# First unit after norms 2 to 6 multiplied with the channel-scaled residual; last two down-projections in one accumulation

## The chip, the cores and the metric

One core of a Trainium2 chip runs the whole program. The metric is the device time of one execution in microseconds (us). The kernel before was timed three times on the chip; one further execution was profiled.

## What is computed

Two layers over 512 tokens (256 latent, 256 context) of 1024 channels, all in float32:

```python
def rms_norm(x, w):
    y = xf * rsqrt(mean(xf * xf, axis=-1) + EPS)      # EPS = 1e-6
    return y * w
def modulate(h, shift, scale): return h * (1 + scale) + shift
def swiglu(h, w13, w2):
    g, u = split(h @ w13, 2)                           # D_FF = 2816
    return (silu(g) * u) @ w2
# per layer, the same weights for latent and context tokens, shift/scale/gate per stream:
x = x + 0.5 * gate1 * swiglu(modulate(rms_norm(x, w1), shift1, scale1), w13a, w2a)
x = x +       gate2 * mixer (modulate(rms_norm(x, w2), shift2, scale2))
x = x + 0.5 * gate3 * swiglu(modulate(rms_norm(x, w3), shift3, scale3), w13b, w2b)
```

The mixer projects to 2576 columns, runs differential attention, windowed attention and a two-directional state-space scan, and projects back. There are six norms: norm 1 at the start, norm 2 before mixer 0, norm 3 before FFN 1, norm 4 before FFN 2, norm 5 before mixer 1, norm 6 before FFN 3. In the code they are n = 0 to 5.

## The kernel before

Tokens lie along the free axis: a tile is 128 channels by 512 tokens, and 1024 channels are KT = 8 tiles, `k` or `d`. Every weight comes as a unit of 128 x 2048 numbers (256 output columns for 8 channel tiles, or 256 hidden rows for a down-projection). SyncE loads a unit into `raw`; ScalarE rounds it to fp32r, `w_hi` (`split`, L527 to L539); VectorE takes the rest, `w_lo` (L872 to L880). TensorE forms each product with three matmuls: high by high, high by low, low by high (`mm3`, L1417). Three slots of `w_hi` and `w_lo` are used in turn.

An FFN has 11 pairs of units: gate, up and down. Gate goes to PSUM banks 0 and 1, up to banks 2 and 3, down to banks 4 to 7 (`4 + d % 4`, so that down tile d + 4 waits until VectorE has added tile d to the residual `x_res`, `update`, L975). The first gate and up units of an FFN stand ahead of its loop (L1449 and L1450). TensorE then runs gate 1, down 0, up 1 and so on. FFN 0 to 2 have 512 tokens, FFN 3 has the 256 latent ones.

A norm runs like this. ScalarE squares a residual tile as soon as it is updated (`norm_square`, L548); VectorE adds the squares (`add_square`, L939). After the last projection one matmul with a matrix of 1/1024 gives the mean in bank 0 (`mean`, L1441). ScalarE loads the table for Ln and Exp, computes the root (L566, L568). Then for each of the 8 tiles VectorE multiplies by the root (L957), ScalarE applies scale and shift for each stream and rounds (L576, L579), and VectorE takes the remainder (L950). TensorE's next unit starts tile by tile as the remainders come.

The order of the work on ScalarE, VectorE and TensorE in a mixer is written out by hand in `WEAVE`, one list for each layer; each engine goes through the list and does what is its own, so an engine that waits holds up all that stands behind it. The lists begin as follows (`T` a projection tile on TensorE, `E` its evacuation by ScalarE, `cv` a convolution on VectorE in five instructions, `S` the split of the next weight unit by ScalarE and VectorE, `R` parts of the decay rows on both):

```
layer 0: cv.0 E.0 E.1 S.0 T0.0 T.2 E.2 R.0 R.1 R.2 E.3 cv.1 T.3 T.4 cv.2 S.1 ... T.5 T.6
layer 1: cv.0 T0.0 cv.1 T.2 E.0 E.1 E.2 R.0 R.1 T.3 T.4 T.5 S.0 E.3 ...
```

T0.0 is the first unit (tiles 0 and 1), T.2 the small dt tile of 16 columns, and T.5 waits for the evacuation E.3 of the tile that held its bank and for its weights (S.0). Ahead of the list both engines wait for the copy of `x_res` to DRAM (`spilled`), since mixer tiles lie in the same memory; SyncE issues that copy after the last multiplication by the root (L404). At the start of FFN 1 VectorE computes two pieces of the modulation vectors (`mod_pieces`, 8 products of 128 x 1024 each), one ahead of the first `split` and `product`, one behind them; the first waits for ScalarE's SiLU of the condition (`cb`, L695), which stands behind norm 3 in ScalarE's order.

## Time and profile before

| | us |
|---|---|
| median of 3 runs | 1903.94 |
| lowest, highest | 1896.11, 1905.94 |
| profiled execution, device time | 1896.38 |
| its span, first to last instruction | 1894.6 |

| Engine | busy us | share of the span |
|---|---|---|
| TensorE matmuls (PE) | 1791.1 | 95% |
| TensorE weight loads (PEld) | 1470.3 | 78% |
| VectorE (DVE) | 1411.0 | 74% |
| ScalarE (ACT) | 722.8 | 38% |

Times in the rows below are us from the start of the span. A timeline row gives start, length, engine, line, output and inputs, the number of instructions merged, and in brackets the idle time before it with what ended it. A matmul's length there includes its way through the array, so in a stream it is longer than the distance from one start to the next. "L1420" and the like are lines of the kernel before.

### The profile page before, as it was taken

The numbers are of one execution on the slowest core, as the hardware profiler recorded it, in microseconds if no ns is written. First come the engines' busy times: TensorE is split into PE (matmuls) and PEld (weight loads), VectorE is DVE, ScalarE is ACT, GpSimd is POOL, SyncE is SP. The second block draws the span as 40 slices with busy tenths as digits, with TensorE's granted clock in tenths as the row PEclk, the third lists the DMA queues.
The fourth block names the chain that finished last, engine by engine and source line by source line (L and its number), as shares of the span: only waits on it lengthen the run. The fifth ranks groups of instructions, "written<-read, shape, count | busy, mean of one in ns | idle before, by whom it ended". The sixth has DMA issues, their size and how long they took to land.

```text
span 1894.6 us, 25682 instructions
## 1 busy us (share of the span) xinstructions
PE 1791.1 (95%) x9154; PEld 1470.3 (78%) x9154; DVE 1411.0 (74%) x2310; ACT 722.8 (38%) x1067; POOL 51.6 (3%) x101
## 2 busy tenths in 40 slices
PE   8999999988999898999999979999999799879999
PEld 5788888866776576788888768888887578569999
DVE  5887777788877757877878657777786788756666
ACT  4322222235656655222222352222223654754342
POOL 1000000000000000000000000000000000000000
PEclk8899999999998898999999989999999899989999
DMA  8444444513312043444443323444440231124542
GB/s 345 177 153 179 153 157 164 185 46 121 123 45 89 1 156 120 180 166 155 165 167 139 128 89 133 155 162 170 155 155 24 111 117 64 71 111 178 179 178 109
DMA packets 37582, 259.43 MB, mean 137 GB/s; under 512 B 4369, under 2 KB 5841, under 8 KB 7441
## 3 DMA queue, kind: packets, MB, share of 16 engines
q1 hardware_dynamic: 26066, 182.32, 26.2%
q0 software_dynamic: 11456, 76.32, 10.9%
q8 instruction: 36, 0.59, 0.1%
q14 instruction: 24, 0.20, 0.0%
HBM read 252.60 MB, written 5.24 MB: 136 GB/s over the span
## 4 chain that ended last, share of the span: by engine, by line
PE 82%; DVE 7%; ACT 7%; issue 2%; DMA 2%; POOL 0%; DVEq 0%; ACTq 0%; SPq 0%; POOLq 0%
PE ps L1420 25%; PE ps L1421 24%; PE ps L1422 24%; ACT n_t L576 2%; PE ps L1485 1%; DVE mod_prod L898 1%; DVE x_res L979 1%; ACT w_hi L532 1%; PE ps L1693 1%; DMA x_spill<-x_res 1%; ACT h_hi L579 1%; DMA scale_w<-scale_in 1%; DVE w_lo L880 1%; PE ps L1635 1%; PE ps L1658 1%
## 5 line engine op out<-in xcount | busy, mean ns | idle before, releaser
L1420 PE MATMUL ps<-h_hi,w_hi 128*128 128x512 f32 (+1 forms) x1872 | 692.0, 370 | 45.2 <-DVE h_lo L950 33.5
L1421 PE MATMUL ps<-h_lo,w_hi 128*128 128x512 f32 (+1 forms) x1872 | 685.9, 366 | 0.0
L1422 PE MATMUL ps<-h_hi,w_lo 128*128 128x512 f32 (+1 forms) x1872 | 685.4, 366 | 0.0
L1420 PEld LDWEIGHTS ps<-h_hi,w_hi 128*128 128x128 f32 x1872 | 357.9, 191 | 116.1 <-issue 44.6
L1422 PEld LDWEIGHTS ps<-h_hi,w_lo 128*128 128x128 f32 x1872 | 357.4, 191 | 58.0
L1421 PEld LDWEIGHTS ps<-h_lo,w_hi 128*128 128x128 f32 x1872 | 357.9, 191 | 56.7 <-issue 0.5
L979 DVE SCALAR_TENSOR_TENSOR x_res<-ps,abg,x_res 128x256 f32<-128x256 f32 x640 | 272.2, 478 | 157.6 <-PE ps L1422 157.1
L875 DVE TENSOR_TENSOR w_lo<-raw,w_hi 128x2048 fp32r<-128x2048 f32 x132 | 302.1, 2288 | 92.5 <-ACT w_hi L532 92.4
L532 ACT ACTIVATE w_hi<-raw 128x2048 fp32r<-128x2048 f32 x132 | 252.2, 1911 | 272.7 <-PE ps L1422 266.4
L898 DVE CUSTOM_DVE_ANT_0 mod_prod<-mod_raw,cb 128x1024 f32<-128x1024 f32 x256 | 301.7, 1220 | 1.6 <-ACT cb L695 1.5
L1420 PE MATMUL ps<-a_hi,w_hi 128*128 128x512 f32 (+1 forms) x640 | 233.3, 365 | 5.7 <-DVE x_res L979 5.7
L1422 PE MATMUL ps<-a_hi,w_lo 128*128 128x512 f32 (+1 forms) x640 | 233.0, 364 | 0.0
L1421 PE MATMUL ps<-a_lo,w_hi 128*128 128x512 f32 (+1 forms) x640 | 233.0, 364 | 0.0
L592 ACT ACTIVATE a_hi<-gu 128x512 fp32r<-128x512 f32 (+1 forms) x80 | 44.2, 579 | 325.8 <-DVE gu L970 325.8
L1420 PEld LDWEIGHTS ps<-a_hi,w_hi 128*128 128x128 f32 x640 | 121.5, 190 | 25.4 <-DVE x_res L979 6.5
L587 ACT ACTIVATE sg<-ps 128x512 f32<-128x512 f32 (+1 forms) x88 | 43.1, 542 | 245.3 <-PE ps L1422 245.3
L1421 PEld LDWEIGHTS ps<-a_lo,w_hi 128*128 128x128 f32 x640 | 121.5, 190 | 18.9
L1422 PEld LDWEIGHTS ps<-a_hi,w_lo 128*128 128x128 f32 x640 | 121.4, 190 | 18.9
L970 DVE TENSOR_TENSOR gu<-ps,sg 128x512 f32<-128x512 f32 (+1 forms) x88 | 50.8, 619 | 65.4 <-PE ps L1422 65.3
L880 DVE TENSOR_TENSOR w_lo<-raw,w_hi 128x2048 fp32r<-128x2048 f32 (+1 forms) x30 | 64.6, 2154 | 13.4 <-ACT w_hi L539 13.3
L450 POOL DMA_DIRECT2D mod_raw<-mod_in x64 | 33.8, 529 | 1217.6 <-DVE mod_acc L898 1007.8
L539 ACT ACTIVATE w_hi<-raw 128x2048 fp32r<-128x2048 f32 (+1 forms) x30 | 53.7, 1801 | 34.6 <-PE ps L1422 29.2
(211 smaller groups left out, 1385.1 us busy)
## 6 DMA issues: line engine op xcount, KB each, us to landing
raw<-ffn_in SPq DMA_DIRECT2D x132, 1024.0 KB, 4.8
mod_raw<-mod_in POOLq DMA_DIRECT2D x68, 1024.0 KB, 5.1
raw<-proj_in SPq DMA_DIRECT2D x20, 1024.0 KB, 5.0
raw<-out_w_in SPq DMA_DIRECT2D x8, 1024.0 KB, 4.8
x_spill<-x_res SPq DMA_DIRECT2D x2, 2048.0 KB, 7.9
x_res<-x_spill SPq DMA_DIRECT2D x2, 2048.0 KB, 7.8
scale_w<-scale_in POOLq DMA_DIRECT2D x4, 512.0 KB, 13.2
x_res<-x_in SPq DMA_DIRECT2D x2, 1024.0 KB, 11.3
```

What stands on the lines that cost most here:

```text
L532: act.activation(w_hi[:, slot, :], raw_of(slot), ACT.Copy).then_inc(hi_ready, 1)
L539: act.activation(w_hi[:, m % 3, 0:n], raw[:, m % 2, 0:n], ACT.Copy).then_inc(hi_ready, 1)
L587: act.activation(sg[:, m, 0:nt], ps[:, m, 0:nt], ACT.Silu).then_inc(silu_done, 1)
L592: act.activation(dst[:, m, 0:nt], gu[:, m, 0:nt], ACT.Copy).then_inc(act_hi_s, 1)
L875: tt(w_lo[:, slot, :], raw_of(slot), w_hi[:, slot, :], ALU.subtract).then_inc(lo_ready, 1)
L880: tt(w_lo[:, m % 3, 0:n], raw[:, m % 2, 0:n], w_hi[:, m % 3, 0:n], ALU.subtract).then_inc(lo_ready, 1)
L898: dve.tensor_tensor_reduce(mod_prod[:, s], mod_raw[:, j // 2, j % 2], cb[:, s, :], 1.0, 0.0, ALU.mult, ALU.add, mod_acc[:, s, j:j + 1]).th ...
L970: tt(gu[:, m, 0:nt], ps[:, 2 + m, 0:nt], sg[:, m, 0:nt], ALU.mult).then_inc(mul_done, 1)
L979: last = stt(out=seg, in0=ps[:, bank, s * LAT:(s + 1) * LAT], scalar=abg[:, n, 2, s, d:d + 1], in1=seg, op0=ALU.mult, op1=ALU.add)
L1420: pe.matmul(dst, w_hi[:, slot, wsl], hi, start=first, stop=False)
L1421: pe.matmul(dst, w_hi[:, slot, wsl], lo, start=False, stop=False)
L1422: return pe.matmul(dst, w_lo[:, slot, wsl], hi, start=False, stop=last)
```

## The change

The normalised tile is root(t) x a(c) x x(c,t) + b(c), with root per token, a and b per channel and stream. The first unit's product is therefore root(t) x (W applied to a x) + (W applied to b).

- ScalarE rounds a x residual (`scaled_high`) right behind each square, VectorE takes the remainder (`scaled_low`) right behind the update, for each tile and stream. After an FFN they go to `h_hi` and `h_lo`, after a mixer to new tiles `u_hi`, `u_lo`.
- TensorE multiplies the first unit with these (`first_unit`), does the mean after the third channel tile (now in bank 3) and, after the sixth, 32 matmuls of 4 columns that apply the unit to the shift (`unit_bias`). The shift's high and low parts come from `split_shift`.
- VectorE multiplies the unit's output by the root in PSUM (`first_scaled`); ScalarE adds the shift's product when it evacuates (`first_evacuation` in a mixer, `silu_first` in an FFN). The norm itself still runs, tile by tile, for the units from the second on.
- The last up unit of an FFN goes ahead of the last but one down unit, and the last two down units run as one accumulation (`last_down`): each residual tile is updated once instead of twice.
- The output projection uses 8 banks. The copy of `x_res` to DRAM is issued after the last update, and its waits move from the head of the mixer to the first writers of the shared memory. The dt tile and tile 3 are interleaved. Weight splits around the norms move.

Cut to its core (the small interfaces, counters and memory layout are left out):

```diff
-                    sp.wait_ge(lo_ready, 3 * base)
+                    sp.wait_ge(lo_ready, 3 * base - 2 if f == 2 else 3 * base)
                     sp.dma_start(raw_of(0), ffn_in[f, 0]).then_inc(raw_in[0], 16)
+                    if f == 2:
+                        sp.wait_ge(lo_ready, 3 * base - 1)
                     sp.dma_start(raw_of(1), ffn_in[f, 1]).then_inc(raw_in[1], 16)
...
-                        sp.wait_ge(t_done, 8 * (3 * layer + 2))
+                        sp.wait_ge(y_evac, updated(2 * layer, LAST_DOWN, KT - 1))
                         sp.dma_start(spill, x_res[:, :, :].rearrange("p k t -> p (k t)")).then_inc(spilled, 16)
...
+            def scaled_high(n, d, nt, dst):
+                act.wait_ge(derive_s, DERIVED_AB[n])
+                for s in streams(nt):
+                    seg = slice(s * LAT, (s + 1) * LAT)
+                    x = act.activation(dst[:, d, seg], x_res[:, d, seg], ACT.Identity, scale=abg[:, n, 0, s, d:d + 1])
+                x.then_inc(u_hi_s, 1)
+
+            def norm_rest(n, nt, first_unit=None, after={}):
...
+                    if first_unit is not None:
+                        act.wait_ge(u_mm, 7 * (n - 1) + min(d + 1, KT - 1))
+                        if d == KT - 1:
+                            act.wait_ge(unit_done, first_unit + 1)
...
+            def silu_first(f, nt):
+                n = NORM_OF_FFN[f]
+                act.wait_ge(bias_done, n)
+                for m in range(2):
+                    act.wait_ge(scaled_s, 2 * n - 1 + m)
+                    act.wait_ge(mul_done, 2 * f * PAIRS - 1 + m)
+                    for s in streams(nt):
+                        seg = slice(s * LAT, (s + 1) * LAT)
+                        x = act.activation(sg[:, m, seg], ps[:, m, seg], ACT.Silu, bias=bias[:, m, s:s + 1])
+                    x.then_inc(silu_done, 1)
...
+                        scaled_high(n, d, ntn, h_hi)
+                    after_last(1)
+                    if f == 1:
+                        norm_rest(n, ntn, base + FFN_UNITS)
+                        after_last(2)
+                        silu_first(f + 1, ffn_tokens(f + 1))
+                    else:
+                        norm_rest(n, ntn, base + FFN_UNITS, after={2: lambda: after_last(2), 5: lambda: first_evacuation(f // 2)})
 
...
-                for q in range(OUT_UNITS):
-                    for d in range(2 * q, 2 * q + 2):
-                        norm_square(n, d, nt, (wo_evac, 8 * layer + d + 1))
-                    split_next(layer, PROJ_UNITS + q + 3)
+                for d in range(KT):
+                    norm_square(n, d, nt, (wo_evac, 8 * layer + d + 1))
+                    scaled_high(n, d, nt, u_hi)
+                    if d in (1, 4, 6):
+                        split_next(layer, MIX_UNITS - 1 + (1, 4, 6).index(d))
                 norm_rest(n, nt)
+                split_next(layer, MIX_UNITS + 2)
+                silu_first(2 * layer + 1, nt)
                 if layer == 0:
...
+            def first_evacuation(layer):
+                n = 3 * layer + 1
+                act.wait_ge(bias_done, n)
+                act.wait_ge(pads, layer + 1)
+                for j in range(2):
+                    act.wait_ge(scaled_s, 2 * n - 1 + j)
+                    for s in range(2):
+                        x = act.activation(xpad[:, j, s, 2:2 + LAT], ps[:, j, s * LAT:(s + 1) * LAT], ACT.Identity, bias=bias[:, j, s:s + 1])
+                    x.then_inc(pj_evac, 1)
...
+            def split_shift(n):
+
+                b = abg[:, n, 1].rearrange("p s k -> p k s")
+                dve.tensor_copy(shift_r[:, :, 0:2], b).then_inc(shift_done, 1)
+                dve.wait_ge(shift_done, 2 * n - 1)
+                tt(shift_r[:, :, 2:4], b, shift_r[:, :, 0:2], ALU.subtract).then_inc(shift_done, 1)
+
+            def scaled_low(n, d, nt, hi, lo):
+                dve.wait_ge(u_hi_s, 8 * (n - 1) + d + 1)
+                for s in streams(nt):
+                    seg = slice(s * LAT, (s + 1) * LAT)
+                    x = stt(out=lo[:, d, seg], in0=x_res[:, d, seg], scalar=abg[:, n, 0, s, d:d + 1], in1=hi[:, d, seg],
+                            op0=ALU.mult, op1=ALU.subtract)
+                x.then_inc(u_lo_s, 1)
+
+            def first_scaled(n, nt, first_unit):
+
+                dve.wait_ge(bias_mm, n)
+                dve.tensor_reduce(bias[:, :, :], ps[:, BIAS_AT, 0:8].rearrange("p (m h s) -> p m s h", m=2, h=2), AX_X,
+                                  ALU.add).then_inc(bias_done, 1)
+                dve.wait_ge(unit_done, first_unit + 1)
+                for m in range(2):
+                    tt(ps[:, m, 0:nt], ps[:, m, 0:nt], n_rstd[:, 0:nt], ALU.mult).then_inc(scaled_s, 1)
+
...
+                        if add_n is not None and 1 <= d < KT - 1:
+                            scaled_low(add_n[0], d - 1, add_n[1], h_hi, h_lo)
...
+                    if f < 3:
+                        derive(NORM_AFTER[f][0], "ab")
+                        split_shift(NORM_AFTER[f][0])
...
-                    norm_rest(nn, ntn, [lambda: after_last(1), lambda: after_last(2)])
-                    if f % 2 == 0:
+                    for d in (KT - 2, KT - 1):
+                        scaled_low(nn, d, ntn, h_hi, h_lo)
+                    after_last(1)
+                    if f == 1:
+                        norm_rest(nn, ntn, {5: lambda: first_scaled(nn, ntn, base + FFN_UNITS)})
+                        after_last(2)
+                    else:
+                        clear_pads()
+                        norm_rest(nn, ntn, {3: lambda: after_last(2), 5: lambda: first_scaled(nn, ntn, base + FFN_UNITS)})
                         derive(nn, "g")
                         derive(nn + 1, "ab")
+                        split_shift(nn + 1)
                 else:
...
+                for d in range(KT):
+                    if d % 2:
+                        dve.wait_ge(unit_done, base + PROJ_UNITS + d // 2 + 1)
+                    else:
+                        dve.wait_ge(o_mm, OUT_UNITS * layer + d // 2 + 1)
+                    update(n, d, d, nt, wo_evac)
+                    if d >= 1:
                         add_square(n + 1, d, nt)
-                    if q < OUT_UNITS - 1:
-                        split_next(layer, PROJ_UNITS + q + 3)
-                norm_rest(n + 1, nt, [lambda: split_next(layer, MIX_UNITS + 2)])
+                    if 1 <= d < 4:
+                        scaled_low(n + 1, d - 1, nt, u_hi, u_lo)
+                    if d >= 3:
+                        scaled_low(n + 1, d, nt, u_hi, u_lo)
+                    if d == 1:
+                        split_next(layer, MIX_UNITS - 1)
+                    elif d == 4:
+                        split_next(layer, MIX_UNITS)
+                split_next(layer, MIX_UNITS + 1)
+                norm_rest(n + 1, nt, {5: lambda: first_scaled(n + 1, nt, base + MIX_UNITS)})
...
+                        dve.wait_ge(spilled, 16 * (layer + 1))
...
-                pe.matmul(ps[:, 0, 0:nt], c_(K_MEAN, P), n_acc[:, 0:nt], start=True, stop=True).then_inc(mean_done, 1)
+                pe.matmul(ps[:, MEAN_AT, 0:nt], c_(K_MEAN, P), n_acc[:, 0:nt], start=True, stop=True).then_inc(mean_done, 1)
+
+            def unit_bias(n, slot):
+
+                pe.wait_ge(shift_done, 2 * n)
+                for m in range(2):
+                    for k in range(KT):
+                        wsl = slice(256 * k + P * m, 256 * k + P * m + P)
+                        pe.matmul(ps[:, BIAS_AT, 4 * m:4 * m + 4], w_hi[:, slot, wsl], shift_r[:, k, :], start=(k == 0), stop=False)
+                        last = pe.matmul(ps[:, BIAS_AT, 4 * m:4 * m + 4], w_lo[:, slot, wsl], shift_r[:, k, :], start=False, stop=(k == KT - 1))
+                last.then_inc(bias_mm, 1)
+
+            def first_unit(n, turn, nt, hi, lo, tile=None):
+
+                split_ready(0, turn)
+                for k in range(KT):
+                    pe.wait_ge(u_lo_s, 8 * (n - 1) + k + 1)
+                    for m in range(2):
+                        last = mm3(ps[:, m, 0:nt], 0, slice(256 * k + P * m, 256 * k + P * m + P), (hi[:, k, 0:nt], lo[:, k, 0:nt]), nt,
+                                   k == 0, k == KT - 1)
+                        if k == KT - 1 and m == 0 and tile is not None:
+                            last.then_inc(tile, 1)
+                    last.then_inc(u_mm if k < KT - 1 else unit_done, 1)
+                    if k == 2:
+                        mean(n, nt)
+                    elif k == 5:
+                        unit_bias(n, 0)
 
...
-                    two_tiles(0, b3, 0, nt, n)
-                    two_tiles(1, b3, 2, nt)
+                    if f == 2:
+                        first_unit(n, b3, nt, h_hi, h_lo)
+                    else:
+                        first_unit(n, b3, nt, u_hi, u_lo)
+                    two_tiles(1, b3, 2, nt, n)
...
+                def last_down():
+
+                    split_ready(1, b3 + LAST)
+                    split_ready(2, b3 + LAST)
+                    parts = [(0, 0), (0, 1), (0, 2), (1, 0), (1, 1), (1, 2)] + [(p, d) for d in range(3, KT) for p in range(2)]
+                    for p, d in parts:
+                        if p == 0:
+                            pe.wait_ge(y_evac, updated(f, LAST_DOWN, d) - 4)
+                        hi, lo = ((a_hi, a_lo), (b_hi, b_lo))[p]
+                        for m in range(2):
+                            if d == 0:
+                                pe.wait_ge(act_lo_s, 2 * (f * PAIRS + LAST - 1 + p) + m + 1)
+                            last = mm3(ps[:, 4 + d % 4, 0:nt], 1 + p, slice(1024 * m + P * d, 1024 * m + P * d + P),
+                                       (hi[:, m, 0:nt], lo[:, m, 0:nt]), nt, p == 0 and m == 0, p == 1 and m == 1)
+                        if p == 1:
+                            last.then_inc(down_done if d < KT - 1 else unit_done, 1 if d < KT - 1 else 2)
+
...
-                two_tiles(1, b3 + LAST, 2, nt)
-                down(0, b3 + LAST, LAST - 1)
-                down(2, b3 + LAST, LAST, b_hi, b_lo)
-                if f < 3:
-                    mean(*NORM_AFTER[f])
+                two_tiles(0, b3 + LAST, 2, nt)
+                last_down()
...
-                        project_dt(layer)
+                        project_dt(layer, range(0, 5))
+                        project(layer, 3, range(0, 5))
+                        project_dt(layer, range(5, KT))
+                        project(layer, 3, range(5, KT))
+                    elif kind == "T" and j == 3:
+                        continue
...
-            for i in range(1, PAIRS):
+            for i in range(1, PAIRS - 1):
                 order += [gate[i], down[i - 1], up[i]]
+            order += [gate[PAIRS - 1], up[PAIRS - 1], down[PAIRS - 2]]
```

## Rows read from the trace of the kernel before

**Rows 1.** Page: busy time of the engines.
```profile
PE 1791.1 (95%) x9154; PEld 1470.3 (78%) x9154; DVE 1411.0 (74%) x2310; ACT 722.8 (38%) x1067; POOL 51.6 (3%) x101
```

**Rows 2.** Waits of TensorE, whole span: total us, times, longest.
```profile
PE ps L1420 <- DVE h_lo L950: 33.5, 11, 6.1
...
PE ps L1420 <- DVE x_res L979: 6.6, 5, 4.5
```

**Rows 3.** Timeline of TensorE around norm 2.
```profile
422.57 1.13 PE L1443 MATMUL ps<-n_acc,const 128*128 128x512 f32 x2 [4.16 <-DVE n_acc L943]
429.75 0.77 PE L1420 MATMUL ps<-h_hi,w_hi 128*128 128x512 f32 x1 [6.06 <-DVE h_lo L950]
...
463.05 0.47 PE L1420 MATMUL ps<-h_hi,w_hi 128*128 128x512 f32 x1 [2.57 <-ACT xpad L725]
```

**Rows 4.** Chain that ended last, at 463 us: start, us, what.
```profile
463.52 0.23 PE ps L1421
```

**Rows 5.** Stages: busy of PE, PEld, DVE, ACT, POOL; granted clock; DMA.
```profile
429.00:434.00 5.00, 4.25 (x10) 3.41 (x11) 4.20 (x7) 4.91 (x10) 0.00 (x0) 0.50 0.01 3
58.00:62.00 4.00, 4.00 (x12) 3.09 (x12) 3.97 (x8) 3.00 (x6) 0.00 (x0) 0.57 0.05 18
```

**Rows 6.** Timeline of ScalarE and VectorE, norm 2 and the head of mixer 0.
```profile
425.61 0.63 ACT L568 ACTIVATE n_rstd<-n_rstd 128x512 f32<-128x512 f32 x1
427.13 1.09 ACT L576 ACTIVATE n_t<-n_t,abg 128x256 f32<-128x256 f32 x2 [0.89 <-DVE n_t L957]
...
428.79 1.08 ACT L576 ACTIVATE n_t<-n_t,abg 128x256 f32<-128x256 f32 x2
...
446.04 0.07 DVE L1070 MEMSET xpad<- 128x8 f32 x1 [3.01 <-DMA x_spill<-x_res]
...
447.07 1.57 DVE L1136 TENSOR_SCALAR cv<-xpad,cols 128x512 f32<-128x512 f32 x1
...
462.33 0.57 ACT L725 ACTIVATE xpad<-ps 128x512 f32<-128x512 f32 x1
```

**Rows 7.** Page: weight splits and residual updates, mean ns of one.
```profile
L979 DVE SCALAR_TENSOR_TENSOR x_res<-ps,abg,x_res 128x256 f32<-128x256 f32 x640 | 272.2, 478 | 157.6 <-PE ps L1422 157.1
L875 DVE TENSOR_TENSOR w_lo<-raw,w_hi 128x2048 fp32r<-128x2048 f32 x132 | 302.1, 2288 | 92.5 <-ACT w_hi L532 92.4
L532 ACT ACTIVATE w_hi<-raw 128x2048 fp32r<-128x2048 f32 x132 | 252.2, 1911 | 272.7 <-PE ps L1422 266.4
```

**Rows 8.** Timeline of TensorE: two bursts of 2-column matmuls near the start.
```profile
54.02 1.84 PE L1755 MATMUL ps<-cond,sg 128*128 128x2 f32 x16
55.72 1.93 PE L1755 MATMUL ps<-cond,gu 128*128 128x2 f32 x16
```

**Rows 9.** Timeline around norm 4: mean, and product of the first up unit.
```profile
1092.08 1.48 PE L1443 MATMUL ps<-n_acc,const 128*128 128x512 f32 x2 [4.16 <-DVE n_acc L943]
...
1126.25 1.29 DVE L970 TENSOR_TENSOR gu<-ps,sg 128x512 f32<-128x512 f32 x2 [5.69 <-PE ps L1422]
```

**Rows 10.** Timeline around norm 5: mean, first convolution, weights of T.5.
```profile
1468.25 2.07 PE L1443 MATMUL ps<-n_acc,const 128*128 128x512 f32 x2 [4.17 <-DVE n_acc L943]
...
1494.14 0.68 DVE L1136 TENSOR_SCALAR cv<-xpad,cols 128x512 f32<-128x512 f32 x1
...
1511.58 0.79 PE L1420 MATMUL ps<-h_hi,w_hi 128*128 128x512 f32 x1 [5.42 <-DVE w_lo L880]
```

**Rows 11.** Timeline around norm 3: mean, first modulation product, first residual update.
```profile
716.12 1.12 PE L1443 MATMUL ps<-n_acc,const 128*128 128x512 f32 x2 [2.37 <-DVE n_acc L943]
...
737.35 1.23 DVE L898 CUSTOM_DVE_ANT_0 mod_prod<-mod_raw,cb 128x1024 f32<-128x1024 f32 x1 [1.47 <-ACT cb L695]
...
765.12 3.23 DVE L979 SCALAR_TENSOR_TENSOR x_res<-ps,abg,x_res 128x256 f32<-128x256 f32 x8 [0.33 <-PE ps L1422]
```

**Rows 12.** Timeline around norm 6: mean, and product of the first up unit.
```profile
1692.06 1.22 PE L1443 MATMUL ps<-n_acc,const 128*128 128x256 f32 x2 [8.61 <-DVE n_acc L943]
...
1713.12 0.76 DVE L970 TENSOR_TENSOR gu<-ps,sg 128x256 f32<-128x256 f32 x2 [0.97 <-PE ps L1422]
```

More of the change, by code:

```diff
@@ L39 @@
 FFN_UNITS = 3 * PAIRS
+DOWNS = PAIRS - 1
+MEAN_AT = 3
+BIAS_AT = 4
 PROJ_UNITS = 11
@@ L128, in backbone @@
         cond = sb(ctx, "cond", [KT, 2])
+        shift_r = sb(ctx, "shift_r", [KT, 4], F32R)
+        bias = sb(ctx, "bias", [2, 2])
         sel_r = sb(ctx, "sel_r", [8, P], F32R)
@@ L713, in evacuate @@
                     act.wait_ge(conv_step, CONV * (6 * layer + j - 1))
-                if what == "cv" and j == 0:
-                    act.wait_ge(pads, layer + 1)
                 if what == "z" and j == 0:
@@ L860, in _ @@
             act.wait_ge(const_in_s, 16)
-            norm_rest(0, T, {1: lambda: split(1, 0, 0), 5: lambda: split(2, 0, 0)})
+            norm_rest(0, T, after={1: lambda: split(1, 0, 0), 5: lambda: split(2, 0, 0)})
             for layer in range(DEPTH):
@@ L959, in norm_rest @@
                         remainder(d - 1)
-                    if d >= KT - len(late):
-                        late[d - KT + len(late)]()
+                    if d in after:
+                        after[d]()
                 remainder(KT - 1)
```

86 lines of the change are left out of this document (36 added, 50 removed).

## The prediction, made before the change was run

> **What bounds the kernel now.** I read the page first: TensorE is busy for 95% of the span [rows 1], so outside its waits it is the bound, and the change takes no matmul away; it adds some. What it can win lies in TensorE's waits. The list of waits says that they end at remainders of norms and, five times, at residual updates [rows 2]. The timelines around the five norms then show what one norm costs. I count from z, the end of the last projection ahead of a norm, which is the start of the mean less the idle time before it: 418.4 for norm 2 [rows 3], 713.75 for norm 3 [rows 11], 1087.9 for norm 4 [rows 9], 1464.1 for norm 5 [rows 10], 1683.45 for norm 6 [rows 12]. At norm 2 TensorE starts its first unit at z + 11.3 [rows 3], and the first ten matmuls come at 0.43 us each, at a granted clock of 0.50, that is 1.2 GHz [rows 5], instead of 0.227 in a stream at 2.4 GHz [rows 4]: 2.0 us more. The reader should then look away from TensorE: what does the first matmul that comes late after the norm wait for? In mixer 0 that is the bank of T.5, at 463.05 [rows 3], in mixer 1 the weights of T.5, at 1511.58 [rows 10]. Both are ends of a serial chain on VectorE and ScalarE, not of TensorE's work.
>
> **Durations.** Six matmuls (one channel tile of a 512-token unit) take 1.36 us, a unit 10.9 [rows 4]. ScalarE's tile step in the norm takes 428.79 less 427.13, 1.65 us, and 8 of them 13.2 [rows 6]; it starts 1.5 us behind the start of Exp [rows 6]. A split costs ScalarE 1.9 and VectorE 2.2 us, a two-stream update 0.9 [rows 7]. `scaled_low` has the form of an update, 0.9 a tile. For `scaled_high` I take the two activations of L576, 1.1 us [rows 6]. Unit_bias is 32 matmuls with a full weight load and 4 columns: 32 of 2 columns take 3.5 us [rows 8].
>
> **After an FFN or mixer: the first unit.** The first weights are split ahead of z in norms 2 to 5, and `scaled_low` of the last tile is done at about z + 3.9: update to 0.9, square to 1.5, `scaled_high` to 2.6, two remainders on VectorE. TensorE needs that tile last, so it runs on without a gap. The mean stands behind three tiles, 4.1 to 4.95. That is the first surprise: the root comes no earlier than before. Exp starts at z + 5.75 (7.2 before [rows 3, 6]), a gain of 1.45 us, and the norm's 13.2 us of tile steps are still all there. After norm 4 a whole split stands ahead of it, and Exp starts at 6.65.
>
> The bias burst costs 3.5 us, and not that alone. Behind the second burst the granted clock is 0.57 over 4 us, and matmuls fall back to 0.43 [rows 5, 8], though the array never stood idle. I charge 2 us of slow matmuls to each burst (0 to 2.8). The first unit then ends at z + 10.9 + 0.85 + 3.5 + 2 = 17.2. The Trainium skill (TensorE: Matmul & The Clock Gate, "HAM oscillation") puts the clock's fall down to the engine standing idle. By that rule a burst without a gap keeps the clock, and the first unit would end 2 us earlier; rows 5 speak against it, and the sum goes by them.
>
> `first_scaled` stands in VectorE's loop behind tile 5. It takes 1.4 us, and waits for the unit's end.
>
> **Norm 2 (mixer 0), nearly nothing.** ScalarE's first tile step starts at z + 7.25. Into its 13.2 us come a split (1.9), a wait of about 1.2 for VectorE's split, four 256-column evacuations (about 1.5), and 1.2 of waiting for `first_scaled`; the last remainder is done at about 25.9. Derive, `split_shift` and the small operations add 2.2: the first convolution starts at z + 28.1. Before, it starts at 447.07, z + 28.65, where the wait for the spill (3.0 us) is in it [rows 6]. So the spill's wait is gone and the norm's longer loop is in its place. From there to E.3, which releases T.5, stay 16.0 us of convolution, split and decay rows (447.07 to 463.05 [rows 3, 6]). T.5 starts 0.5 us earlier against z, and 0.3 more because the stall between the last down units is gone (rows 2 hold three such, with 4.5 and 1.2 us elsewhere). But TensorE is done with T.4 at z + 34, not 42, and stands for 10 us instead of 2.6, so the clock falls, which it did not at 463 [rows 4], and ten matmuls cost 2.0 us more. Net **+1.2 us**.
>
> **Norm 5 (mixer 1), a little.** The same working, but the convolution started at z + 30.05 before [rows 10]: 1.9 us earlier, and 0.3. The slow restart is there already. **-2.2 us**.
>
> **Norm 4 (FFN 2), the full gain.** Before, the up unit's product starts at z + 38.3 [rows 9]. After: the first unit ends at 17.2, the second at 28.1; its tiles are ready in time (the last at about 23.5). ScalarE, with tile 6 held up by `first_scaled`, ends the norm at 22.7, then split 1.9, a table load 1.3, `silu_first` about 1.8: 27.7, just ahead. **-10.1 us** and 0.3, -10.4.
>
> **Norm 3 (FFN 1), a loss.** This is where the order turns against the change. TensorE again gets through its second unit at 28.1. But the two modulation pieces on VectorE wait for `cb`, and ScalarE now has a split, the SiLU table and `silu_first` between the norm and `cb`. Before, the first piece starts at 737.35, z + 23.6 [rows 11]. After: norm 22.7, split 24.6, table 25.9, `silu_first` 27.7, `cb` 2.0: z + 29.8. All that follows up to the first residual update, 27.8 us later at 765.12, is VectorE's serial work [rows 11], and TensorE's down unit cannot pass its fourth tile without that update; before, it waited 1.2 us there. So the whole 6.2 us shift is on the path, and the longer stall (about 8 us) lowers the clock: 1.9 more. **+8.1 us**. The first unit's early start is given back in full.
>
> **Norm 6 (FFN 3), even.** TensorE's matmuls are half as long, and the splits don't fit under them. I follow VectorE: the split of the first unit ends at about z + 2.1, so TensorE starts there; the mean waits for the last square until about z + 8.1; the clock is low by then, and the burst at that clock costs up to twice 3.5. The first unit ends between z + 18 and z + 23 and the third starts at z + 26 to 30 (before 29.7 [rows 12]); VectorE's chain in the first down unit takes 1.9 back. From -2.5 to +2.5, I take **-0.5**.
>
> **The rest.** VectorE is spared 24 tile updates of 0.9 us and 8 of half that, and gets 32 and 8 half `scaled_low`; ScalarE gets as many `scaled_high` of 1.1 us [rows 6, 7]. All of it runs under TensorE's projections, which give 2.7 us a tile there, where it isn't counted above. The last accumulation ends where the two did, since TensorE's matmuls there are the same.
>
> **Sum.** 1.2 - 2.2 - 10.4 + 8.1 - 0.5 = -3.8 us. The profiled execution of 1896.4 would take 1892.6. The median of the runs lies 7.5 us above that execution, so the time to expect is 1903.9 - 3.8 = 1900. About 0.5%, 9.5 us, is what a measurement of this kernel can tell from no change.
>
> **Rivals.**
> - The mixers follow TensorE. If T.5 came when T.4 is done, at z + 34, norm 2 would give 12 us more and norm 5 11 us: 1877. For it speaks that the spill's wait is gone; against it the unchanged 16 and 17.4 us from the first convolution to T.5 [rows 3, 6, 10]. Chance 0.13.
> - Small terms all fall well: activations with one pointer operand at 0.35 instead of 0.55 us, the clock holding behind the bursts and through part of the stalls. Norm 3 gives 3 less, norm 4 and 6 give 2 more each, norm 2 gives 2: 1891. Chance 0.2.
> - Slower than before: the bursts. At the low clock a small matmul takes twice its time. If the burst takes 7.1 us and leaves twice as many slow matmuls, the first unit ends at z + 22.8. In the mixers `first_scaled`, otherwise due at 19.4, then waits 3.4 us and everything behind it too; in norms 3, 4 and 6 the shift is 5.6, 5.6 and 4. Together 22 us: 1922. It decides once the first unit ends later than z + 19.4. Against it: in norms 2 to 5 TensorE has run without a gap when the burst begins. Chance 0.12.
> - The first unit doesn't start at z, because a split or a last remainder is late. In norms 2 and 5 it would change nothing, in norm 4 each us counts: 1900 to 1906. Chance 0.1, within 0.5%.
>
> The forecast has 0.45. Faster by over 0.5%: 0.33, the first two. Slower by over 0.5%: 0.18, the burst and a longer chain at norm 3. Within: 0.49. The range of 8 in 10 goes from 1880 to 1912; the forecast's own from 1893 to 1906.
>
> **What the profile would show.** TensorE without a gap at z, then a row of 32 short matmuls of about 0.11 us and slow ones behind. The first convolution of mixer 0 at z + 28 (z + 18 would make me wrong, towards faster). A wait of about 10 us before T.5 in both mixers, a granted clock of 0.5 behind it. The first modulation product at z + 30, and a wait for `x_res` of about 8 us in FFN 1's first down unit: without it norm 3 is a gain. At norm 4, 28 us from z to the third unit.

## The result, and the profile after

| | us |
|---|---|
| after, median (lowest, highest) | 1888.78 (1888.54, 1891.49) |
| before, median (lowest, highest), executions beside it | 1896.41 (1895.89, 1905.94) |
| ratio after to before, 95% interval | 0.9942, 0.9921 to 0.9964 |
| profiled execution after, its span | 1888.78, 1887.1 |
| profiled execution before, its span | 1896.38, 1894.6 |

The change makes the kernel 0.58% faster. Between the two profiled executions it is 7.6 us; the prediction's sum was 3.8. The kernel before has times in two groups, 1895 to 1900 and 1903 to 1907 us; the profile that the prediction read is of the lower one (the experiment before_again shows the upper). The median of the table lies in the lower group by chance: of all 77 executions of the kernel before beside the changed kernel and the experiments, 44 are in the upper one, and their median is 1904.1 us. So against a lower execution the change gains some 7.6 us, against an upper one some 15; what follows explains the first number.

Page of after, busy time of the engines [rows 1 before]:

```profile
PE 1811.9 (96%) x9314; PEld 1496.1 (79%) x9314; DVE 1423.3 (75%) x2351; ACT 752.0 (40%) x1147; POOL 51.6 (3%) x101
```

TensorE is busy 20.8 us longer, though the span is 7.5 us shorter. So about 28 us of waits went, and nearly three quarters of that was paid back in added and slowed matmuls. Waits of TensorE in after, whole span: total us, times, longest [rows 2]:

```profile
PE ps L1514 <- DVE x_res L1056: 12.5, 3, 6.6
...
PE ps L1514 <- DVE w_lo L933: 10.4, 1, 10.4
PE ps L1514 <- ACT xpad L776: 8.6, 1, 8.6
...
PE ps L1514 <- DVE a_lo L1050: 3.7, 1, 3.7
```

The wait for the mean stood at 23.5 us before:

```profile
PE ps L1443 <- DVE n_acc L943: 23.5, 5, 8.6
```

Nearly all of it is gone (2.5 are left, at norm 6), and so are the 33.5 us for remainders of the norm [rows 2]. In their place stand x_res and a_lo (FFN 1) and the two waits of T.5. Timeline of TensorE at norm 2 [rows 3]:

```profile
420.03 1.02 PE L1537 MATMUL ps<-n_acc,const 128*128 128x512 f32 x2
...
425.00 0.17 PE L1545 MATMUL ps<-shift_r,w_hi 128*128 128x4 f32 x1
425.03 0.25 PE L1546 MATMUL ps<-shift_r,w_lo 128*128 128x4 f32 x1
...
428.49 0.73 PE L1514 MATMUL ps<-h_hi,w_hi 128*128 128x512 f32 x1
429.02 0.63 PE L1515 MATMUL ps<-h_lo,w_hi 128*128 128x512 f32 x1
...
459.39 0.76 PE L1514 MATMUL ps<-h_hi,w_hi 128*128 128x512 f32 x1 [8.63 <-ACT xpad L776]
```

No idle time stands before the mean. Three channel tiles take 4.08 us, so z is the mean's start less 4.08: 415.95 here. The row of 32 small matmuls takes 3.5 us. Of the full ones behind it eight come at 0.43 us. T.5 comes at z + 43.4 behind a wait of 8.6 us. Norm 3, VectorE and TensorE [rows 11], and norm 5, VectorE and TensorE [rows 10]:

```profile
740.39 1.22 DVE L951 CUSTOM_DVE_ANT_0 mod_prod<-mod_raw,cb 128x1024 f32<-128x1024 f32 x1 [2.48 <-ACT cb L738]
...
754.15 0.80 PE L1514 MATMUL ps<-a_hi,w_hi 128*128 128x512 f32 x1 [3.67 <-DVE a_lo L1050]
...
768.14 2.05 DVE L1056 SCALAR_TENSOR_TENSOR x_res<-ps,abg,x_res 128x256 f32<-128x256 f32 x5 [0.33 <-DVE abg L990]
...
769.07 0.79 PE L1514 MATMUL ps<-a_hi,w_hi 128*128 128x512 f32 x1 [6.57 <-DVE x_res L1056]
...
1485.25 0.49 DVE L1229 TENSOR_SCALAR cv<-xpad,cols 128x512 f32<-128x512 f32 x1
...
1502.47 0.80 PE L1514 MATMUL ps<-h_hi,w_hi 128*128 128x512 f32 x1 [10.39 <-DVE w_lo L933]
```

To see where the time goes I take one marker for each FFN, the product of gate and up (gu) in its second pair, from where on both kernels run alike to the last turn. Before, then after:

```profile
113.39 1.29 DVE L970 TENSOR_TENSOR gu<-ps,sg 128x512 f32<-128x512 f32 x2 [2.71 <-PE ps L1422]
782.92 1.29 DVE L970 TENSOR_TENSOR gu<-ps,sg 128x512 f32<-128x512 f32 x2 [0.17 <-issue]
1159.09 1.29 DVE L970 TENSOR_TENSOR gu<-ps,sg 128x512 f32<-128x512 f32 x2 [1.15 <-PE ps L1422]
1730.60 0.75 DVE L970 TENSOR_TENSOR gu<-ps,sg 128x256 f32<-128x256 f32 x2 [1.55 <-PE ps L1422]
```

```profile
111.69 1.29 DVE L1047 TENSOR_TENSOR gu<-ps,sg 128x512 f32<-128x512 f32 x2 [2.38 <-PE ps L1516]
787.90 1.29 DVE L1047 TENSOR_TENSOR gu<-ps,sg 128x512 f32<-128x512 f32 x2 [2.13 <-PE ps L1516]
1153.04 1.29 DVE L1047 TENSOR_TENSOR gu<-ps,sg 128x512 f32<-128x512 f32 x2 [1.15 <-PE ps L1516]
1723.25 0.76 DVE L1047 TENSOR_TENSOR gu<-ps,sg 128x256 f32<-128x256 f32 x2 [1.54 <-PE ps L1516]
```

The lead of after is 1.7, -5.0, 6.05 and 7.35 us. With z of each norm between them (415.95, 711.5, 1092.1, 1457.3, 1674.5 after) it splits up so (us, minus is a gain; "measured" is one execution of each kernel):

| stretch | predicted | measured |
|---|---|---|
| start-up, to FFN 0's second pair | 0 | -1.7 |
| last turns of the four FFNs | -0.9 | -2.5 |
| norm 2 and mixer 0 | +1.5 | +0.2 |
| norm 3 | +8.1 | +7.2 |
| norm 4 | -10.1 | -10.3 |
| norm 5 and mixer 1 | -1.9 | -2.1 |
| norm 6 | -0.5 | +1.6 |
| sum | -3.8 | -7.5 |

### The profile page after: what moved, and what is told of

Read it like the earlier page. It is cut to its first block, busy times and chain, and to the rows that moved or that the text cites. A ratio compares the mean times of both kernels' runs of the same rounds, so it can differ in the third digit from the quotient of the medians.

```text
span 1887.1 us, 26111 instructions
## 1 busy us (share of the span) xinstructions
PE 1811.9 (96%) x9314; PEld 1496.1 (79%) x9314; DVE 1423.3 (75%) x2351; ACT 752.0 (40%) x1147; POOL 51.6 (3%) x101
## 4 chain that ended last, share of the span: by engine, by line
PE 84%; DVE 6%; ACT 6%; issue 3%; DMA 1%; POOL 0%; ACTq 0%; DVEq 0%; POOLq 0%
PE ps L1514 25%; PE ps L1515 25%; PE ps L1516 25%; PE ps L1622 1%; DVE mod_prod L951 1%; ACT w_hi L546 1%; ACT n_t L598 1%; PE ps L1830 1%; DMA scale_w<-scale_in 1%; PE ps L1772 1%; PE ps L1891 1%; PE ps L1795 1%; DVE x_res L1056 1%; PE ps L1805 1%; PE ps L1645 1%
## 5 line engine op out<-in xcount | busy, mean ns | idle before, releaser
L1514 PE MATMUL ps<-h_hi,w_hi 128*128 128x512 f32 (+1 forms) x1840 | 680.3, 370 | 26.3 <-DVE w_lo L933 10.4
L1515 PE MATMUL ps<-h_lo,w_hi 128*128 128x512 f32 (+1 forms) x1840 | 673.7, 366 | 0.0
L1516 PE MATMUL ps<-h_hi,w_lo 128*128 128x512 f32 (+1 forms) x1840 | 672.9, 366 | 0.0
L1514 PEld LDWEIGHTS ps<-h_hi,w_hi 128*128 128x128 f32 x1840 | 350.5, 190 | 90.7 <-issue 22.9
L1516 PEld LDWEIGHTS ps<-h_hi,w_lo 128*128 128x128 f32 x1840 | 350.2, 190 | 57.4
L1515 PEld LDWEIGHTS ps<-h_lo,w_hi 128*128 128x128 f32 x1840 | 350.6, 191 | 56.6 <-issue 1.2
L1056 DVE SCALAR_TENSOR_TENSOR x_res<-ps,abg,x_res 128x256 f32<-128x256 f32 x584 | 248.4, 477 | 151.2 <-PE ps L1516 150.2
```

The costliest lines, as they stand in the source:

```text
L1056: last = stt(out=seg, in0=ps[:, bank, s * LAT:(s + 1) * LAT], scalar=abg[:, n, 2, s, d:d + 1], in1=seg, op0=ALU.mult, op1=ALU.add)
L1514: pe.matmul(dst, w_hi[:, slot, wsl], hi, start=first, stop=False)
L1515: pe.matmul(dst, w_hi[:, slot, wsl], lo, start=False, stop=False)
L1516: return pe.matmul(dst, w_lo[:, slot, wsl], hi, start=False, stop=last)
```

## Experiments

Leads and losses of single stretches below are differences of the same gu markers, with each execution's own start-up taken off.

**last_down_only.** The kernel before with `last_down` alone (the diff's lines of it, and the next splits moved):

```
-                down(0, b3 + LAST, LAST - 1)
-                down(2, b3 + LAST, LAST, b_hi, b_lo)
+                last_down()
...
+                    if f == 1:
+                        after_last(1)     # both behind norm_rest
+                        after_last(2)
```

> The kernel before with one part of the change alone: the last two down units of each FFN as one accumulation (the splits of the next units 1 and 2 go behind the squares, after norm 4's loop in FFN 1). The prediction counted 0.3 us at three norms and nothing in FFN 3, 0.9 in all: 1895.5 against 1896.4. What the two traces show at z (0.77, 0.78 and 0.75 us gained in the last turns of FFN 0, 1 and 2, 0.2 in FFN 3) would make it 2.5: 1893.9.

Measured: median 1891.09 us, ratio to before 0.9947 (0.9927 to 0.9967). The four last turns give 0.61, 0.60, 0.59 and 0.19 us, 2.0 in all. Norm 4 gives another 2.9, which was not expected. Timeline of TensorE at norm 4 in it:

```profile
1088.15 2.08 PE L1452 MATMUL ps<-n_acc,const 128*128 128x512 f32 x2 [2.36 <-DVE n_acc L948]
```

The mean waits 2.36 us behind z instead of 4.16 [rows 9]. Before, an update and a sum of squares take VectorE 1.39 us a tile in the last down unit and TensorE 1.36, so VectorE ends late; with one accumulation TensorE takes 2.72 us a tile. That is 1.8 of the 2.9 us. The rest may be the split that no longer stands ahead of the root; no run separates it. So the simplest part of the change, without a first unit, gives 4.4 of the 5.8 us that remain without start-up.

**n3_cb.** What holds FFN 1's start? ScalarE's SiLU of `cb` moved from behind `silu_first` to ahead of the squares of norm 3.

> The changed kernel with one step moved: ScalarE takes the SiLU of cb ahead of the squares of norm 3 instead of behind silu_first. Theory 1, the prediction's: FFN 1's start is set by VectorE's serial work that waits for cb. Then VectorE goes straight from the third split into the modulation products, the first of them comes 2.5 us earlier (the wait of 2.48 us for cb in the changed kernel's trace is gone), TensorE's wait for x_res falls from 6.6 to about 4.1 us, and the time is 2.5 us lower, 1886.3 us. Rival: norm 3 loses by the extra work of TensorE (mean, bias burst, slow matmuls); then the products come earlier, TensorE's end does not, and the time stays at 1888.8.

Measured: 1890.65 us, and 3.4 us worse than after at norm 3: neither theory. ScalarE and TensorE in it:

```profile
690.65 2.01 ACT L730 ACTIVATE cb<-cb 128x1024 f32<-128x1024 f32 x2 [4.36 <-DMA cb<-c_in]
...
721.11 2.08 PE L1537 MATMUL ps<-n_acc,const 128*128 128x512 f32 x2 [3.21 <-DVE n_acc L996]
```

The wait of 2.48 us for `cb` went as expected, but a wait of 4.36 for the data of `cb` came in, and with it every square and every update of the mixer's end was late, so that the mean waited. A step was moved to where ScalarE was idle, but ahead of its own input.

**n3_piece.** As n3_cb, and two modulation products in the norm's loop:

```
+                    late[6] = lambda: (dve.wait_ge(cb_ready, 6), mod_tile(MOD_PRE[1][0], 0))
```

> As n3_cb, and the first quarter of the first modulation piece goes into VectorE's norm loop, behind tile 6. Theory 1: VectorE's serial chain to the first residual update loses another 2 to 3 us of idle time between norm tiles, so the first update comes about 5 us earlier than in the changed kernel (768.1 us from the start), TensorE starts down unit 0 without a wait for a_lo (3.7 us now) and with it one slow restart fewer (1.9 us): 5 to 7.5 us lower in all, about 1882.5. Rival, TensorE's own work: no change, 1888.8. Slower, about 1890, if the last remainder comes so late that the up unit waits for it.

Measured: 1890.3 us; 0.4 better than n3_cb at norm 3. Behind tile 6 the two products push the last multiplication by the root back, and the split behind it as well, so most of what they save in the chain is lost. The late `cb` is in it too.

**n3_gap.** The same step, placed behind its data:

```
                     if d in (1, 4, 6):
                         split_next(...)
+                    if layer == 0 and d == 1:
+                        act.wait_ge(cb_in_s, 32)   # and the two SiLU activations
```

> The SiLU of cb again ahead of norm 3, now behind the split after tile 1, where ScalarE stands idle for 3.15 us in the changed kernel and the data of cb has landed (in n3_cb it stood ahead of tile 0, waited 4.4 us for the data, and held up every square behind it). Theory 1, VectorE's chain behind cb sets the start of FFN 1: the chain loses the wait of 2.48 us, x_res is waited for 4.1 us instead of 6.6, and FFN 1's products from the second on come 2.5 us earlier against the first FFN's: 1886.3 us. Rival, TensorE's extra work sets it: 1888.8.

Measured: 1886.74 us. At norm 3 it gains 2.66 us against after: theory 1, with the size it gave. The first update comes 2.3 us earlier. But the sign named for it did not come: the wait for x_res rose to 9.2 us instead of falling to 4.1, while the wait for a_lo in front of it fell from 3.7 to 1.1. The two together are as long as in after (10.3 and 10.2 us). What shortened is the stretch of slow matmuls between them: after the short wait TensorE runs its first tiles of the down unit at full clock, reaches the fourth tile sooner and stands there for longer. So the time of the update tells the gain, and the length of the wait does not. In the total this execution also has norm 6 3.0 us cheaper, and norm 4 and mixer 1 1.6 and 1.0 us dearer; all three are far from the edit.

**n3_gap_piece.** n3_gap, with the two products at `late[7]` instead, between the last multiplication by the root and the last remainder.

> As n3_gap, with two of the 16 modulation products between the last multiplication by the root and the last remainder of norm 3, where VectorE is idle for 0.96 and 1.11 us. Theory 1: another 2 us of the chain go, the wait for a_lo is gone and with it one row of slow matmuls: 4.5 to 6.5 us less than the changed kernel, about 1883.5. Rival: 1888.8.

Measured: 1883.18 us (1881.5 to 1883.81), ratio to before 0.9897 (0.9866 to 0.9928): the best of all kernels run. VectorE and TensorE:

```profile
734.33 1.22 DVE L951 CUSTOM_DVE_ANT_0 mod_prod<-mod_raw,cb 128x1024 f32<-128x1024 f32 x1
...
764.89 3.22 DVE L1056 SCALAR_TENSOR_TENSOR x_res<-ps,abg,x_res 128x256 f32<-128x256 f32 x8 [0.33 <-DVE abg L990]
...
765.82 0.79 PE L1518 MATMUL ps<-a_hi,w_hi 128*128 128x512 f32 x1 [8.37 <-DVE x_res L1056]
```

3.8 us less than after at norm 3, and the wait for a_lo is gone. Its profiled execution has another 3.0 at norm 6, of which bias_spread tells. Even here TensorE waits 8.4 us for the first update: VectorE's chain is still the bound.

**bias_spread.** The same 32 small matmuls in three parts:

```
-                    elif k == 5:
-                        unit_bias(n, 0)
+                    elif 4 <= k <= 6:
+                        unit_bias(n, 0, k - 4)
```

> The changed kernel with the 32 small matmuls of unit_bias in three parts of 10, 10 and 12, behind channel tiles 4, 5 and 6, instead of one row of 32 behind tile 5. The work is the same. Theory, the prediction's: it is the unbroken row of small matmuls that costs the clock. Then no matmul at 0.43 us follows, the first unit ends 1.9 us earlier at each norm, and the time falls by 1.9 at norm 4, 1 to 2 at norm 6 and nothing at norms 2, 3 and 5, where VectorE's chain decides: about 1885.8. Rival: the share of small matmuls in the stretch counts, not their being in one row; then the slow matmuls stay and so does the time, 1888.8.

Measured: 1886.17 us. Stages at norm 2, after and then bias_spread (busy PE, PEld, DVE, ACT, POOL; granted clock; DMA):

```profile
425.00:430.00 5.00, 5.00 (x37) 4.71 (x36) 3.46 (x5) 4.94 (x8) 0.98 (x2) 0.85 0.91 320
430.00:435.00 5.00, 5.00 (x20) 3.03 (x18) 4.19 (x5) 3.56 (x8) 0.00 (x0) 0.80 0.32 107
```

```profile
425.00:430.00 5.00, 5.00 (x34) 4.47 (x34) 3.46 (x5) 4.94 (x8) 0.99 (x2) 1.00 0.90 323
430.00:435.00 5.00, 4.60 (x20) 2.10 (x19) 4.19 (x4) 3.57 (x8) 0.00 (x0) 1.00 0.31 90
```

The clock holds at 1.00. The other traces agree: in the two kernels with the spread row no slow matmuls follow it at norms 2 to 5, in the nine with the unbroken row six to twelve follow it at 34 of these 36 norms. The two exceptions are norm 3 in mix0_nogap and in head_light; what was different there is open. That the row's being unbroken counts, and not the share of small matmuls, is not shown, since three parts with full matmuls between them also thin the small ones out. What the spreading is worth is less than expected. At norm 4 0.5 us is left of 1.9, since TensorE now waits for `silu_first`; at norm 2 TensorE waits for the norm instead. Norm 6 takes 3.0 us less in it, but that is not shown to be of the spread row: of the eleven kernels with a first unit seven have the cheap norm 6, six of them with the unbroken row, three, after among them, have the dear one, and best lies between. Stage of 16 us behind the mean of norm 6, after and then bias_spread:

```profile
1682.00:1698.00 16.00, 16.00 (x73) 15.82 (x74) 8.75 (x19) 8.19 (x16) 0.00 (x0) 0.50 0.19 67
```

```profile
1682.00:1698.00 16.00, 15.98 (x97) 15.80 (x98) 9.99 (x21) 11.08 (x20) 0.00 (x0) 0.70 0.20 67
```

**mix0.** Are the mixers' heads bound by order or by amount of work?

```
-  "... S.0 T0.0 T.2 E.2 R.0 R.1 R.2 E.3 cv.1 T.3 T.4 cv.2 S.1 R.3 E.4 E.5 si.0 cv.3 S.2 si.1 si.2 si.3 ..."
+  "... S.0 T0.0 T.2 E.2 R.0 E.3 cv.1 T.3 T.4 E.4 S.1 cv.2 E.5 si.0 cv.3 S.2 si.1 si.2 si.3 E.6 E.7 R.1 R.2 R.3 ..."
```

> The changed kernel with mixer 0's written order altered for ScalarE and VectorE: the evacuation E.3, the second convolution, S.1, cv.2, cv.3 and S.2 go ahead of the decay rows R.1 to R.3. TensorE's order is the same. The prediction says that T.5 is late because of the serial chain on VectorE and ScalarE, not because of TensorE. If so, T.5 starts when T.4 ends, at 450.8 instead of 459.4, and no slow matmuls follow it. What is left of these 8.6 and 1.5 us at the end: if only T.5 was late, 8 to 10 us, 1880; if VectorE's whole work up to the rotations bounds the head of the mixer, the stall comes back at t.4, c.0 or the tiles behind them, and 0 to 3 us are left: 1886 to 1889. Likelier is the second, since VectorE has no gap from 444.5 to 483.

Measured: 1893.11 us, slower than after. T.5's wait is gone, and a wait is back further on (VectorE's idle time ahead of the decay rows, and TensorE's ahead of t.0):

```profile
472.30 0.68 DVE L1277 TENSOR_TENSOR rows<-rows 16x512 f32<-16x512 f32 x1 [2.41 <-ACT rows L859]
...
487.35 1.12 PE L1622 MATMUL ps<-const,cv 128*128 128x128 f32 x4 [4.75 <-ACT cv L817]
```

VectorE's first normalisation, the last piece of the head, starts at 488.9 instead of 483.3: my order made VectorE wait for ScalarE three times (2.47, 0.97 and 2.41 us). Mixer 0 is 3.3 us longer. The waits alone don't make that: TensorE comes to t.0 8.3 us ahead of after, waits 4.8 and 1.3 us there, and is still 2.2 us ahead. Behind these waits the clock is low where after has 1.00, and that costs 5.5 us:

```profile
489.00:494.00 5.00, 4.23 (x12) 2.95 (x12) 4.97 (x6) 4.80 (x7) 3.10 (x6) 0.50 0.42 107
494.00:499.00 5.00, 5.00 (x19) 3.67 (x19) 3.44 (x7) 4.64 (x6) 0.00 (x0) 0.50 0.63 211
```

**mix1.** The same for mixer 1, S.0 first.

> The same for mixer 1: S.0 ahead of the convolutions, E.3 right behind the first one, the decay rows R.1 to R.3 behind cv.3 and S.2. T.5 waits 10.4 us for its weights in the changed kernel, because VectorE's part of S.0 stands behind 7 us of decay rows. Expected: T.5 at 1492 instead of 1502.5. Of the 10.4 and 1.9 us, all is left if TensorE has enough other work before it needs the decay rows (1877), 0 to 4 us if the stall comes back (1885 to 1889). Here VectorE has less to do behind the head, since the mixer's output is for 256 tokens: 4 to 6 us, about 1884.

Measured: 1894.39 us. The wait of 10.4 us for T.5's weights turned into this one ahead of t.0:

```profile
PE ps L1622 <- ACT cv L817: 12.7, 1, 12.7
```

At its end TensorE is 3.0 us behind after, and the low clock behind it (0.52 from 1530 to 1535 us, after 1.00 in that work) makes most of the rest: mixer 1 is 6.6 us longer.

**mix0_nogap.** mix0 with ScalarE's S.1 ahead of E.4, S.2 ahead of E.5, and its Ln of R.1 behind E.3.

> mix0 again, without the idle time that its order gave VectorE (2.47, 0.97 and 2.41 us of waits for ScalarE): ScalarE takes S.1 ahead of E.4, S.2 ahead of E.5, and its Ln of the decay rows right behind E.3. VectorE's last piece of head work, the first normalisation, is then due at 483 us as in the changed kernel (488.9 in mix0). Theory: VectorE's amount of work bounds the head of the mixer, so TensorE's early T.5 is given back in a stall ahead of t.4 or c.0: at most 4 us less, minus up to 2 us of slow matmuls behind that stall: 1885 to 1889. Rival: mix0 was slower only by its own gaps, and T.5's 8.6 us are there to be had: 1880.

Measured: 1891.80 us, but spread from 1888.0 to 1894.06. Without VectorE's gaps the head is shorter: at the start of the attention (its first Copy of z) the lead over after is 4.5 us, a little more than expected. At the end of the mixer it is a loss of 3.2: the clock stands at 0.50 for 20 us in between, with TensorE busy nearly throughout:

```profile
640.00:645.00 5.00, 5.00 (x9) 1.99 (x8) 2.25 (x9) 2.55 (x6) 0.00 (x0) 0.50 0.00 0
645.00:650.00 5.00, 4.22 (x13) 2.44 (x13) 2.26 (x8) 1.56 (x5) 0.00 (x0) 0.50 0.00 0
650.00:655.00 5.00, 5.00 (x24) 3.04 (x26) 2.35 (x9) 3.68 (x10) 0.00 (x0) 0.50 0.00 0
655.00:660.00 5.00, 5.00 (x22) 2.94 (x18) 1.36 (x7) 1.23 (x4) 0.00 (x0) 0.54 0.00 0
```

So both theories were half right. With T.5 early and no slow matmuls behind it TensorE is 10.4 us ahead of after when it comes to t.0. There it waits 2.6 us for the convolutions of VectorE and ScalarE, and the low clock behind that wait (0.55 from 485 to 490 us) costs 3.2, which leaves 4.5. The stretch at 640 us takes those again, and 3.2 more.

**head_light.** Six small VectorE steps (1.7 us) moved out of each head to behind x.0.

> The changed kernel with the derive steps and split_shift of the next norm (six small VectorE instructions, 442.00 to 443.72 us in the changed kernel) moved from the head of each mixer to behind the first state step, x.0. Theory, as it stands after mix0 and mix1: VectorE's amount of work bounds the head of both mixers. Then the first convolution and all behind it come 1.7 us earlier, and the time falls by 1.7 us for each mixer, to 1885.4. Rival: the head is bound by ScalarE or TensorE, and the time stays at 1888.8.

Measured: 1885.82 us, as expected in sum and wrong in place. The first convolution comes only 0.8 us earlier in mixer 0, not 1.7, T.5's waits fell by 0.8 and 1.1 us, and both mixers end as in after to 0.1 us. In mixer 0 TensorE's lead of 0.8 us is 0.4 behind the slow matmuls of T.5 and gone behind the slow ones of the attention. All 3.0 us of the profiled execution lie at norm 6, so the agreement with the expected time is luck, and the theory was not borne out.

**best.** n3_gap_piece, bias_spread and head_light in one kernel.

> n3_gap_piece, bias_spread and head_light together. By their traces the first saves 3.8 us at norm 3 against the changed kernel, the spread row 0.5 at norm 4 and about 2.5 at norm 6, the lighter head 3.4 if its theory holds: 1878.6 us from 1888.8. If the parts share a bound (norm 3's chain starts earlier by what mixer 0 gives, so they should not), less: 1882.

Measured: 1886.60 us (1885.22 to 1887.75), no better than its parts and worse than n3_gap_piece. Up to the end of FFN 2 the parts add up: it leads after by 4.6 us, n3_gap_piece by 3.8. Then mixer 1 takes 2.9 us more than in after, in a stretch z + 167 to z + 177, where after and n3_gap_piece have the full clock:

```profile
1620.00:1625.00 5.00, 3.71 (x13) 1.75 (x11) 3.97 (x11) 3.08 (x8) 0.00 (x0) 0.85 0.00 0
1625.00:1630.00 5.00, 5.00 (x25) 3.29 (x25) 1.57 (x5) 2.56 (x9) 0.00 (x0) 0.50 0.00 0
```

Norm 6 takes 2.0 us more than in n3_gap_piece, too.

**before_again.**

> The kernel before, profiled once more. Its times lie in two groups, 1895 to 1900 us and 1904 to 1907, and the profile that the prediction read is of the lower one. If this execution falls in the upper group, its trace shows where the 9 us lie. Expected: one stretch where a stall between two updates or ahead of a norm lets the clock fall and it then stays at 0.50 for some 9 us more, as at norm 6, where the changed kernel and its variants differ by 2.5 us in that way. Rival: many small shares.

Measured: 1902.9 us, the upper group. All markers agree with the first profile to 0.3 us up to norm 2 and then stand 6.5 us later to the end. Stages of mixer 0's attention:

```profile
600.00:640.00 40.00, 31.96 (x182) 19.18 (x178) 31.56 (x65) 27.77 (x70) 0.00 (x0) 0.82 0.00 1
640.00:660.00 20.00, 19.22 (x64) 10.53 (x65) 9.52 (x30) 9.15 (x24) 0.00 (x0) 0.55 0.00 0
660.00:680.00 20.00, 20.00 (x105) 12.98 (x106) 11.40 (x36) 12.05 (x34) 0.00 (x0) 0.94 0.00 1
```

It is one stretch: 64 matmuls in 20 us at 0.55, where the first profile has 106 at 1.00. The list of TensorE's waits is the same in both to 0.1 us. In the 3.8 us ahead of the fall, 638 to 641.8, TensorE is busy for 2.88 us here and 2.89 in the first profile, and the clock is 1.00 in both.

## Why the prediction was right or wrong

The time lies in the range of 1880 to 1912 us, and the sign of every large term was right. It lies outside the forecast's own 1893 to 1906; the forecast "within 0.5%" was missed by 0.1%, and the sum was half of what was measured. Term by term:

- **Norm 4, right**: -10.1, measured -10.3. The second unit follows the first without a wait, and `silu_first` is just in time (it ends at z + 27.3; gu comes at z + 31.3 behind a split, but TensorE has no wait for it).
- **Norm 3, right in mechanism and size**: +8.1, measured +7.2. The first modulation product came at z + 28.9 (predicted 29.8), the first update 5.3 us later than before (6.2), and n3_gap and n3_gap_piece show that this chain and not TensorE sets it. Only the wait was split in two, 3.7 for a_lo and 6.6 for x_res, each with its slow restart (2.7 and 2.1 us), instead of one of 8 with 1.9.
- **Norms 2 and 5, right in mechanism**: first convolution at z + 28.6 and 28.0 (28.1), T.5's waits 8.6 and 10.4 (10), clock 0.5 behind them. Mixer 0 came out 1.3 better. T.5 came at z + 43.4 instead of 44.1: from the first convolution to it stood 14.9 us, not 16.0, since the first convolution's first step took 0.49 us, not the 1.57 of before (why is open). The slow matmuls behind T.5 cost 1.6 us instead of 2.0.
- **Last turns, undersized**: 0.3 us each at three norms, measured 0.77, 0.77, 0.75 and 0.19. The step that failed is "the stall between the last down units is gone" priced by the wait for x_res alone, and FFN 3 put at nothing. The kernel before shows what the row leaves out:

```profile
411.97 0.39 PE L1422 MATMUL ps<-b_hi,w_lo 128*128 128x512 f32 x1
412.67 0.50 PE L1420 MATMUL ps<-b_hi,w_hi 128*128 128x512 f32 x1 [0.31 <-DVE x_res L979]
413.01 0.39 PE L1421 MATMUL ps<-b_lo,w_hi 128*128 128x512 f32 x1
```

  From start to start it is 0.70 and 0.34 us here against 0.227 in the stream, 0.58 more in all for a wait of 0.31; last_down_only measures 0.6. The other 0.16 us at each norm is no gain: z before is the end of a matmul, with its way through the array, and z after is a start.
- **Norm 6, wrong sign**: -0.5, measured +1.6. The range of 2.5 to either side held it. The burst came at the low clock, as feared there, and the clock stayed at 0.50 for the whole stage. There the row of small matmuls takes 6.7 us. In seven of the eleven kernels, n3_gap_piece and head_light among them, with the same work at norm 6, the norm is 3.0 us cheaper, which is -1.4; so neither sign is shown for the change.
- **Start-up, -1.7**: not in the sum, and not of the change; the first product comes between 75.4 and 77.4 us in the kernels run, which are alike up to there.
- **From the span to the median**: I added 7.5 us because before's median lay above its profiled execution. That was the weakest step. 6.5 of them are a low-clock stretch in mixer 0's attention (before_again). The seven executions of after lie within 3 us, so they don't carry over to it. That the change is what took them away is not shown: mix0_nogap, which has the change in it, shows such a stretch. From the profile alone, 1892.6, the error is 3.8 us; from the median 11.

Of the rivals, "the mixers follow TensorE" is refuted as it stood: T.5 comes at z + 43.4 and not z + 34, and an order with T.5 early gives 4.5 us in the head of mixer 0, not 12. "Small terms all fall well" names the nearest time, 1891, but not by its terms: norm 3 gave 0.9 and not 3, norm 4 0.2 and not 2, and norm 6 went the other way. The slower one, row of small matmuls at the low clock, held only at norm 6. "The first unit doesn't start at z" did not come at norms 2 to 5, where no idle time stands before the mean. The Trainium skill (TensorE: Matmul & The Clock Gate, "HAM oscillation") puts the fall of the clock down to idle stretches; here eight matmuls at 0.43 us follow a row without any gap, and with the row spread none does, so the rule does not cover this case, and the rows 5 that spoke against it were the right guide.

Open: why a stretch of mixer attention falls to the low clock in one execution and not in another, why norm 6 has two costs, and what norm 4's 2.9 us in last_down_only owe to the split.

## What to carry to other kernels

When TensorE's idle time at a norm is filled with work from the other side of the norm, look for the engine whose chain comes next: here three quarters of the 28 us of removed waits were paid back. Before a step is moved to where its engine is idle, look up when its input lands (n3_cb against n3_gap: 6.1 us). Compare kernels stretch by stretch with markers that both have: gains of 2 to 3 us in the total can lie in a clock stretch far from the edit (head_light), and a gain at the edit can be hidden by one (mix0_nogap, best). Count the slow matmuls behind a wait with it: where a reordering moves a wait and does not remove it, they come along (mix0, mix1).

## What the runs showed of the hardware

- A gapless row of 32 matmuls of 4 columns (3.5 us) is followed by eight full ones at 0.43 us (clock 0.80 in that stage); the same matmuls in parts of 10, 10 and 12 leave the clock at 1.00. In all traces slow matmuls follow the unbroken row at 34 of 36 norms of 512 columns, the spread one at 0 of 8.
- In the attention, where TensorE issues 100 to 130 small matmuls in 20 us at full clock, the clock stands at 0.50 for up to 20 us in some executions and costs 6.5 us (before_again), with the same waits and TensorE as busy before the fall as in the execution that kept the clock (2.88 and 2.89 of 3.8 us). The Trainium skill (TensorE: Matmul & The Clock Gate, "What's actually happening") says that the count of slow matmuls varies from run to run of one kernel; the runs agree, but with a cost of 0.34% here and not only at the start.
- The same norm 6 with the same work costs up to 3.0 us more or less by how long the clock stays low behind its two stalls (mean 0.50 or 0.7 in the stage shown at bias_spread); seven of eleven kernels have the cheap form.
- Two waits of TensorE cost more than the idle time in their rows: 0.58 us from start to start for 0.31 us at full clock (last turn of FFN 0, kernel before), and 2.7 us of slow matmuls on top of the 3.7 us for a_lo in after.
